# One core, two-layer trunk: two chunks of expert scores moved into the rank stage, one-hot products spread over 123 chunks, first expert loads moved into the gates stage

## The chip, the cores and the metric

The kernel runs on 1 core of one Trainium2 chip. The metric is the device time of one execution in microseconds (us), median over runs. TensorE (PE in the profile) does the matrix products, PEld is its weight load, VectorE (DVE), ScalarE (ACT) and GpSimd (POOL) do the elementwise work, and SyncE (SP) issues most of the DMA transfers. The kernel is written in five instruction streams, one for each engine, which meet only at semaphores and at the end of each stage: a stage is one block, and no engine starts the next block before all five have ended this one.

## The reference, cut to what matters

Two layers; each has a token mixer and then a PEER layer, which is where the change lies. There are 512 latent tokens and, in layer 0 alone, 256 context tokens as well. D is 1024, and there are 16384 experts on a grid of 128 x 128 keys.

```python
def peer_ffn(h, w_q, keys, u_tab, v_tab):
    q = (h @ w_q).reshape(bn, t, PEER_HEADS, 2, PEER_HALF)
    s = jnp.einsum('bthcd,hckd->bthck', q, keys)
    s_top, i_top = lax.top_k(s, PEER_TOPK)                       # rank stage
    cand_s = s_top[..., 0, :, None] + s_top[..., 1, None, :]
    cand_i = i_top[..., 0, :, None] * PEER_NKEYS + i_top[..., 1, None, :]
    best_s, pos = lax.top_k(cand_s.reshape(...), PEER_TOPK)      # gates stage: "select"
    idx = jnp.take_along_axis(cand_i, pos, axis=-1)
    gates = jax.nn.softmax(best_s, axis=-1)
    pre = einsum('ced,cd->ce', u_tab[idx], h)                    # 16 experts a head, 8 heads
    act = jax.nn.gelu(pre)
    return einsum('ce,ced->cd', act * gates, v_tab[idx])
```

## The kernel before

Of the tokens of a layer, most blocks of 128 are "dense": all 16384 expert activations are computed for them and multiplied by a gate that is zero for all but 128 experts. Layer 0 has 4 dense blocks (512 tokens) and 2 sparse ones, layer 1 has 3 dense ones (384 tokens) and 1 sparse. For sparse blocks only the chosen rows of the tables are gathered.

**stage_rank** makes the 16 query tiles and their scores on PE and ranks them on DVE. `t.product(pe, i, s, ...)` is one tile of product: 8 steps k, each of three matmuls (high weights by high tokens, high by low, low by high). ACT rounds a weight tile to its high part (`t.hi`), POOL in this stage, DVE in the next, makes the low part (`t.lo`); a product waits for `lo_done`, and for `acc_free`, which ACT gives when it has emptied the accumulator two tiles before.

**stage_gates** runs over 128 chunks c of 128 experts of the table u, of 8 steps each, so over 1024 positions p = 8c + k. All engines' streams are written out along p. At position p:

- PE does step k of chunk c, and ahead of it, at the positions of `group_at`, one group of 8 one-hot matmuls (L1124), which scatter the gates of 4 tokens into a 128 x 128 grid. `turn` (L1115) transposes the selections of a block, 12 positions ahead of the block's first group.
- DVE makes `low(c + 2)` where k = 0, the one-hots of the group that comes 14 positions later (L1008), a share of the row dots of the sparse blocks (`dots_to`, L985), and between these, in 13 pieces, the "select" of the block that `order` says (L1029 to L1096).
- ACT, after chunk c: `ahead(c)`, a gelu of the accumulator (L1146) that waits until the spill of chunk c - 2 has landed, then `hi(c + 3)`. Eight positions ahead of a group it scales the one-hots (`ojg`, L1160), two positions behind it copies the product to `stage` (L1169).
- SP loads the weight tile of chunk c + 4 (L131), stores 8 groups of gates at once (L1242, 2 MB), and spills chunk c's activations to `act_dram` (L1253). It is one queue in program order: a DMA whose issue takes long, or a wait, holds all behind it.

The groups start at chunk `lead` (16 and 20), and a block has `per` chunks (28 and 36), so the groups stand 7 positions apart in layer 0 and 9 in layer 1, and the last at position 1020 and 1019. At the end SP waits for all stores and spills.

**stage_experts** multiplies the activations by the gates (DVE, L1402), splits them (ACT L1374, DVE L1407) and multiplies them by the 128 chunks of the table v (PE, L1352 to L1354). It starts with SP's `quad_load(0)` (gates of the first 4 chunks, 1 MB in layer 0) and `act_load` of chunks 0 and 1. DVE also adds the gathered rows of v for the sparse blocks (L1416), which POOL fetches (L1333) after a memset (L1329).

## Time and profile before

| | us |
|---|---|
| median of the runs (4388.56 to 4394.6, 3 runs) | 4391.62 |
| the profiled execution, its own time | 4389.09 |
| its span in the trace | 4387.4 |
| PE busy in the span | 4032.8 (92%) |
| DVE busy in the span | 3231.5 (74%) |

The span is what the trace covers, the own time is measured around it. From the trace's rows, the stages of the PEER layer lie so: rank ends at about 662 and 3108, gates ends at about 1542 and 3794, experts ends at about 2279 and 4364.

### The profile page before, as it was taken

Reading aid. Unit: us, or ns where it says so; the run is one execution under the profiler, and the core shown is the slowest. Engines: PE = TensorE matmul, PEld = TensorE weight load, DVE = VectorE, ACT = ScalarE, POOL = GpSimd, SP = SyncE. Lnnn points to the kernel's source line nnn. Section 1 sums busy time; section 2 is a strip of 40 time slices with the busy share of each in tenths; the row PEclk is TensorE's granted clock in tenths of the full one; section 3 lists DMA queues with packets and bytes.
Section 4 is the critical chain, followed back from the end, with each engine's and each line's share of the span. In section 5 each row is a group of like instructions: output and inputs, shape, how many; then the busy total and the mean of one; then the engine's idle time right before and its main releaser. Section 6 shows DMA issues by size and latency. Waiting matters only on the chain. (4 is left out here: it accounts for less than half of the span.)

```text
span 4387.4 us, 62475 instructions
## 1 busy us (share of the span) xinstructions
PE 4032.8 (92%) x20380; PEld 3434.4 (78%) x20380; DVE 3231.5 (74%) x5929; ACT 1947.7 (44%) x3694; POOL 1163.9 (27%) x906
## 2 busy tenths in 40 slices
PE   8997788999999989999987999888799999899998
PEld 2776577788888868888866877656789999899997
DVE  2694588999897778888875455546887877577777
ACT  2111224777777722222224434323367778533332
POOL 0232121343343244444422111112122222122221
PEclk9998899999999999999998999889899999999999
DMA  7441115899999899999951111012378888899996
GB/s 278 169 168 58 44 43 183 284 326 335 318 344 332 316 386 375 373 374 376 376 196 49 38 38 39 29 48 77 123 270 285 285 281 300 293 333 333 331 336 213
DMA packets 411888, 1026.08 MB, mean 234 GB/s; under 512 B 33968, under 2 KB 182448, under 8 KB 405680
## 3 DMA queue, kind: packets, MB, share of 16 engines
q1 hardware_dynamic: 297648, 608.42, 39.0%
q0 software_dynamic: 110592, 402.70, 25.7%
q10 hardware_dynamic: 3456, 12.58, 0.9%
q8 instruction: 98, 1.61, 0.1%
q14 instruction: 94, 0.77, 0.1%
HBM read 904.03 MB, written 119.54 MB: 233 GB/s over the span
## 5 line engine op out<-in xcount | busy, mean ns | idle before, releaser
L136 ACT ACTIVATE w_hi<-w_raw 128x1024 fp32r<-128x1024 f32 x536 | 568.1, 1060 | 1197.9 <-PE psum L1354 879.8
L168 PE MATMUL psum<-h_hi,w_hi 128*128 128x512 f32 (+1 forms) x2208 | 876.4, 397 | 140.3 <-DMA keysr<-in_peer_keys 50.0
L169 PE MATMUL psum<-h_lo,w_hi 128*128 128x512 f32 (+1 forms) x2208 | 840.4, 381 | 0.0
L170 PE MATMUL psum<-h_hi,w_lo 128*128 128x512 f32 (+1 forms) x2208 | 839.7, 380 | 0.0
L147 DVE TENSOR_TENSOR w_lo<-w_raw,w_hi 128x1024 fp32r<-128x1024 f32 x424 | 519.5, 1225 | 413.3 <-ACT w_hi L136 392.2
L1352 PE MATMUL psum<-a_hie,w_hi 128*128 128x512 f32 (+1 forms) x2048 | 764.4, 373 | 30.7 <-DVE a_loe L1407 30.7
L1354 PE MATMUL psum<-a_hie,w_lo 128*128 128x512 f32 (+1 forms) x2048 | 751.6, 367 | 0.0
L1353 PE MATMUL psum<-a_loe,w_hi 128*128 128x512 f32 (+1 forms) x2048 | 750.0, 366 | 0.0
L1228 POOL DMA_INDIRECT u_rowsg<-in_peer_u_rows,expert_idx x384 | 443.4, 1155 | 1099.9 <-DVE u_rowsg L985 974.2
L1333 POOL DMA_INDIRECT v_rowse<-in_peer_v,expert_idx x384 | 421.4, 1097 | 828.2 <-DVE row_sume L1416 815.0
L1160 ACT ACTIVATE ojg<-eq_jg,gate_Tg 128x128 fp32r<-128x128 bf16 x1792 | 546.9, 388 | 167.5 <-DVE eq_jg L1008 166.6
L147 POOL TENSOR_TENSOR w_lo<-w_raw,w_hi 128x1024 fp32r<-128x1024 f32 x116 | 289.4, 2495 | 1145.2 <-ACT w_hi L136 1145.2
L168 PEld LDWEIGHTS psum<-h_hi,w_hi 128*128 128x128 f32 x2208 | 425.9, 193 | 195.5 <-issue 84.4
L1416 DVE SCALAR_TENSOR_TENSOR row_sume<-v_rowse,expert_weight,row_sume 128x1024 f32<-128x1024 f32 x384 | 491.4, 1280 | 0.1
L170 PEld LDWEIGHTS psum<-h_hi,w_lo 128*128 128x128 f32 x2208 | 424.3, 192 | 64.8
L985 DVE SCALAR_TENSOR_TENSOR u_rowsg<-u_rowsg,psum 128x1024 f32<-128x1024 f32 x384 | 463.1, 1216 | 9.5 <-DMA u_rowsg<-in_peer_u_rows,expert_idx 6.4
L169 PEld LDWEIGHTS psum<-h_lo,w_hi 128*128 128x128 f32 x2208 | 425.8, 193 | 49.0 <-issue 12.9
L1352 PEld LDWEIGHTS psum<-a_hie,w_hi 128*128 128x128 f32 x2048 | 385.7, 188 | 93.6 <-DVE a_loe L1407 31.8
L1354 PEld LDWEIGHTS psum<-a_hie,w_lo 128*128 128x128 f32 x2048 | 385.7, 188 | 50.4
L1353 PEld LDWEIGHTS psum<-a_loe,w_hi 128*128 128x128 f32 x2048 | 386.1, 189 | 45.9
L1124 PEld LDWEIGHTS psum<-ojg,eq_ig 128*128 128x128 f32 x1792 | 230.9, 192 | 78.8 <-ACT ojg L1160 70.1
L1124 PE MATMUL psum<-ojg,eq_ig 128*128 128x128 f32 x1792 | 232.6, 273 | 50.1 <-ACT ojg L1160 49.9
(228 smaller groups left out, 5740.2 us busy)
## 6 DMA issues: line engine op xcount, KB each, us to landing
w_raw<-in_peer_u SPq DMA_DIRECT2D x256, 512.0 KB, 5.9
w_raw<-in_peer_v SPq DMA_DIRECT2D x256, 512.0 KB, 5.5
gates<-stageg SPq DMA_DIRECT2D x28, 2048.0 KB, 15.7
acts<-act_gg SPq DMA_DIRECT2D x128, 256.0 KB, 5.0
gte<-gates SPq DMA_DIRECT2D x32, 1024.0 KB, 8.3
act_fe<-acts SPq DMA_DIRECT2D x128, 256.0 KB, 6.3
ada_w<-in_ada_w SPq DMA_DIRECT2D x12, 2048.0 KB, 8.2
ada_rows<-in_ada_w SPq DMA_DIRECT2D x48, 512.0 KB, 3.4
```

Of the source, the lines that this page charges most:

```text
L136: act.activation(self.weights(s)[0], self.raw[:, slot, :], ACT.Copy).then_inc(self.hi_done, 1)
L147: pool.tensor_tensor(lo, self.raw[:, slot, :], hi.bitcast(F32), ALU.subtract).then_inc(self.lo_done, 1)
L168: pe.matmul(out, wh, hi[:, k], start=(k == 0), stop=False)
L169: pe.matmul(out, wh, lo[:, k], start=False, stop=False)
L170: last = pe.matmul(out, wl, hi[:, k], start=False, stop=(k == KC - 1))
L985: dve.scalar_tensor_tensor(out=row, in0=row, scalar=1.0, in1=h_row, op0=ALU.mult, op1=ALU.mult, accum_out=pre_act[:, s, r:r + 1]).then_inc ...
L1124: last = pe.matmul(t.psum[:, 4 + g % 2, j * P:(j + 1) * P], eq_i[:, g % EQ, j], oj[:, g % OJ, x, j], start=(x == 0), stop=(x == 1))
L1160: last = act.activation(oj[:, g % OJ, x, j], eq_j[:, g % EQ, j], ACT.Copy, scale=gate_T[:, b % 2, x, r + j:r + j + 1])
L1352: pe.matmul(out, vh, a_hi[:, s], start=(begin and i == 0), stop=False)
L1353: pe.matmul(out, vh, a_lo[:, s], start=False, stop=False)
L1354: last = pe.matmul(out, vl, a_hi[:, s], start=False, stop=(end and i == QUAD - 1))
L1416: dve.scalar_tensor_tensor(out=acc[:, s], in0=vbuf[:, slot], scalar=weight[:, s, bass.ds(c, 1)], in1=acc[:, s], op0=ALU.mult, op1=ALU.add) ...
```

## The change

Three edits, in both layers.

1. At the end of stage_rank PE makes chunks 0 and 1 of the gates stage, over the dense tokens only: chunk 0 between the last query tile and the last scores, chunk 1 behind these. The PE loop of stage_gates starts at chunk 2. The work of ACT, DVE and SP for chunks 0 and 1 stays in stage_gates.
2. The groups of one-hot products are spread evenly from chunk `lead` to chunk 123: `span` is 856 positions for 128 groups in layer 0, which is 6.7 apart (before 7), and 824 for 96 groups in layer 1, 8.6 apart (before 9). The last group stands at 980 and 978; no group stands in the last five chunks. The ends of the selects move with the blocks: in layer 0 those behind the first dense block end at positions 199, 326, 540 and 754 (before 202, 336, 560 and 784).
3. The buffer `stage` now lives through both stages, and the expert stage's gate and activation buffers lie in it. SP, 12 positions behind the last store, waits until all stores have landed and then issues the loads of the first quad of gates and of activations 0 and 1, which stage_experts issued before.

```diff
+TAIL = 5
+ACTS = 4
...
                 for i in range(n - BODY, n):
                     if i + 1 < n:
                         t.product(pe, i + 1, (i + 1) % SPLIT, t.moving(tokens))
+                    else:
+                        t.wide = 1
+                        t.product(pe, n, 0, t.moving(tokens - S * P))
                     scores(i, i)
+                t.product(pe, n + 1, 1, t.moving(tokens - S * P))
+                t.wide = 2
...
-    per = (NKEYS - lead) // dense
     GB = P // 4
-    gap = per * KC // GB
+    span = (NKEYS - TAIL - lead) * KC
...
         def start(b):
-            return (lead + b * per) * KC
+            return lead * KC + b * span // dense
         def at(g):
-            return start(g // GB) + g % GB * gap + gap // 2
+            return lead * KC + g * span // (dense * GB) + 3
...
-                for c in range(NKEYS):
+                for c in range(SPLIT, NKEYS):
...
+                n = dense * STAGES
+                last_store = at(dense * GB - 1) + 4
                 for p in range(END):
                     if p % KC == 0:
                         load(p // KC + RAW)
+                    if p == last_store + 12:
+                        for x in range(2):
+                            sp.wait_ge(stored[x], 16 * (n // 2 + 1))
+                            sp.wait_ge(spilled[x], 32)
+                        gt, act_t = expert_buffers(stage, Td)
+                        sp.dma_start(gt[:, 0], g_dram[0].rearrange("i n x -> i (n x)")).then_inc(g_in, 16)
+                        for x in range(2):
+                            sp.dma_start(act_t[:, x], act_dram[x]).then_inc(act_in[x], 16)
...
-                if at(dense * GB - 1) + 4 >= END:
-                    store(dense * GB - 1)
-                n = dense * STAGES
                 for x in range(2):
                     sp.wait_ge(spilled[x], 16 * (NKEYS // 2 + 1))
-                    sp.wait_ge(stored[x], 16 * (n // 2 + 1))
...
+def expert_buffers(stage, Td):
+    halves = [stage[:, x].rearrange("p n x -> p (n x)") for x in range(2)]
+    return (halves[0][:, 0:2 * QUAD * Td].rearrange("p (a x) -> p a x", a=2),
+            halves[1][:, 0:ACTS * Td].rearrange("p (a x) -> p a x", a=ACTS))
...
                 sp.sem_inc(alo_done, A)
                 sp.sem_inc(gated, QUAD + 1)
-                quad_load(0)
-                act_load(0, 0)
-                act_load(1, 1)
```

On PE, at the end of layer 0's rank stage, before the change (L779 are the scores, L168 to L170 the three matmuls of a step, `hc_hip` and `hc_lop` the context tokens; the branches mark the change of block):

```order
L170 MATMUL psum<-hc_hip,w_lo 128x256
L779 MATMUL psum<-keysr,qTr 128x128 x12
L747 UNCONDITIONAL_BRANCH
L1107 UNCONDITIONAL_BRANCH
L168 MATMUL psum<-h_hi,w_hi 128x512
L169 MATMUL psum<-h_lo,w_hi 128x512
L170 MATMUL psum<-h_hi,w_lo 128x512
```

The same place with the change (lines are two higher there; the first "..." leaves out the rest of chunk 0, the second that of chunk 1):

```order
L172 MATMUL psum<-hc_hip,w_lo 128x256
L781 MATMUL psum<-keysr,qTr 128x128 x6
L170 MATMUL psum<-h_hi,w_hi 128x512
...
L781 MATMUL psum<-keysr,qTr 128x128 x6
L170 MATMUL psum<-h_hi,w_hi 128x512
...
L749 UNCONDITIONAL_BRANCH
L1113 UNCONDITIONAL_BRANCH
L170 MATMUL psum<-h_hi,w_hig 128x512
```

The 24 matmuls of chunk 0 now stand ahead of the last 6 score products and those of chunk 1 behind them, both ahead of the block's end; the next block starts with chunk 2, whose weights are in `w_hig` and `w_log`.

On SP, at the end of layer 0's gates stage and the start of its expert stage, before the change (`acts` are the spills, `gates` the stores, `gte` and `act_fe` the expert stage's loads):

```order
L1253 DMA acts<-act_gg 128x512
L131 DMA w_raw<-in_peer_v 128x1024
L1253 DMA acts<-act_gg 128x512
L1242 DMA gates<-stageg 128x32x128
L958 UNCONDITIONAL_BRANCH
L1291 UNCONDITIONAL_BRANCH
L1300 DMA gte<-gates 128x2048
L1295 DMA act_fe<-acts 128x512 x2
```

The same queue with the change, from the last store on (the spills are L1266, the first loads of the expert stage L1257 and L1259, its other loads of activations L1310):

```order
L1245 DMA gates<-stage 128x32x128
L1266 DMA acts<-act_gg 128x512
L133 DMA w_raw<-in_peer_v 128x1024
L1257 DMA stage<-gates 128x2048
L1259 DMA stage<-acts 128x512 x2
L1266 DMA acts<-act_gg 128x512
...
L133 DMA w_raw<-in_peer_v 128x1024
L1266 DMA acts<-act_gg 128x512
L964 UNCONDITIONAL_BRANCH
L1306 UNCONDITIONAL_BRANCH
```

The last store moved ahead of the last five spills, and the three loads now stand behind the store and the spill of chunk 123, and ahead of the spills of chunks 124 to 127.

## Rows read from the trace of the kernel before

**Rows 1.** The page: busy time, share of the span, instructions.
```profile
PE 4032.8 (92%) x20380; PEld 3434.4 (78%) x20380; DVE 3231.5 (74%) x5929; ACT 1947.7 (44%) x3694; POOL 1163.9 (27%) x906
```

**Rows 2.** Windows, gates stages: us, busy and count by engine, PE clock, DMA.
```profile
725.00:750.00 25.00, 19.55 (x85) 15.38 (x83) 24.07 (x51) 11.25 (x12) 8.77 (x6) 0.98 0.67 230
1425.00:1450.00 25.00, 25.00 (x127) 21.13 (x127) 22.18 (x34) 21.19 (x55) 9.09 (x9) 1.00 0.99 356
```

**Rows 3.** Windows, experts stage, layer 0.
```profile
2000.00:2050.00 50.00, 50.00 (x216) 40.23 (x215) 43.00 (x45) 14.23 (x18) 20.59 (x18) 1.00 0.99 379
```

**Rows 4.** Timeline of PE, rank to gates: start, us, [idle before <-releaser].
```profile
662.18 0.77 PE L168 MATMUL psum<-h_hi,w_hi 128*128 128x512 f32 x1 [15.78 <-PEq L747]
...
3108.24 0.66 PE L168 MATMUL psum<-h_hi,w_hi 128*128 128x384 f32 x1 [17.72 <-PEq L747]
```

**Rows 5.** Timeline, gates to experts, both layers.
```profile
1543.93 0.94 POOL L1333 DMA_INDIRECT v_rowse<-in_peer_v,expert_idx  x1 [0.15 <-issue]
1547.63 0.75 DVE L1402 TENSOR_TENSOR act_fe<-act_fe,gte 128x512 f32<-128x512 f32 x1 [11.45 <-DMA act_fe<-acts]
1549.83 0.80 PE L1352 MATMUL psum<-a_hie,w_hi 128*128 128x512 f32 x1 [17.30 <-DVE a_loe L1407]
...
3799.23 0.56 DVE L1402 TENSOR_TENSOR act_fe<-act_fe,gte 128x384 f32<-128x384 f32 x1 [8.36 <-DMA act_fe<-acts]
3800.99 0.69 PE L1352 MATMUL psum<-a_hie,w_hi 128*128 128x384 f32 x1 [13.35 <-DVE a_loe L1407]
```

**Rows 6.** Timeline of ACT, start of layer 0's gates stage.
```profile
664.63 1.28 ACT L1146 ACT_TABLE_LOAD   x1
670.14 0.60 ACT L1146 ACTIVATE act_gg<-psum 128x512 f32<-128x512 f32 x1 [4.23 <-PE psum L170]
670.91 1.06 ACT L136 ACTIVATE w_hi<-w_raw 128x1024 fp32r<-128x1024 f32 x1 [0.17 <-ACT act_gg L1146]
...
703.12 0.60 ACT L1146 ACTIVATE act_gg<-psum 128x512 f32<-128x512 f32 x1 [3.62 <-PE psum L170]
...
708.56 0.60 ACT L1146 ACTIVATE act_gg<-psum 128x512 f32<-128x512 f32 x1 [3.62 <-PE psum L170]
```

**Rows 7.** Timeline of DVE, first microseconds of the gates stages.
```profile
664.89 1.22 DVE L147 TENSOR_TENSOR w_log<-w_raw,w_hig 128x1024 fp32r<-128x1024 f32 x1
672.08 1.23 DVE L147 TENSOR_TENSOR w_lo<-w_raw,w_hi 128x1024 fp32r<-128x1024 f32 x1 [3.35 <-ACT w_hi L136]
...
699.60 1.23 DVE L147 TENSOR_TENSOR w_log<-w_raw,w_hig 128x1024 fp32r<-128x1024 f32 x1 [1.41 <-ACT w_hig L136]
...
3117.29 1.23 DVE L147 TENSOR_TENSOR w_lo<-w_raw,w_hi 128x1024 fp32r<-128x1024 f32 x1 [2.50 <-ACT w_hi L136]
```

**Rows 8.** Waits, 725 to 775 us: who <- whom, total, times, longest.
```profile
PE psum L1115 <- DVEq L1097: 7.6, 1, 7.6
```

**Rows 9.** Groups of instructions: the one-hot products (busy, mean | idle before).
```profile
L1124 PE MATMUL psum<-ojg,eq_ig 128*128 128x128 f32 x1792 | 232.6, 273 | 50.1 <-ACT ojg L1160 49.9
```

**Rows 10.** Line L958, end of both gates stages: count, duration, first to last start.
```profile
L958 DVEq DRAIN x2: 17/17/17, 1536.5 to 3791.1; - x2
L958 SPq DRAIN x2: 7/7/7, 1541.7 to 3794.0; - x2
```

**Rows 11.** Timeline of SP and ACT around a store, layer 0.
```profile
1486.77 0.45 SPq L1242 DMA_DIRECT2D gates<-stageg  x1
1492.09 11.26 SPq L1253 DMA_DIRECT2D acts<-act_gg  x1
...
1509.17 0.60 ACT L1146 ACTIVATE act_gg<-psum 128x512 f32<-128x512 f32 x1 [4.25 <-DMA acts<-act_gg]
```

**Rows 12.** Stores (L1242) from issue to landing: layer 0, all 16.
```profile
DMA to landing us min/median/max: 7.9/18.7/21.4
```

**Rows 13.** The same in layer 1, without its last store (11).
```profile
DMA to landing us min/median/max: 10.1/10.8/14.1
```

**Rows 14.** First gather of v (L1333, issued at 1543.93), to landing.
```profile
DMA to landing us min/median/max: 6.3/6.3/6.3
```

More of the change, by code:

```diff
@@ L871, in stage_rank, with stage_gates @@
         t.end_stage(n, RAW)
-def stage_gates(t, layer, tokens, top, top_i, h_tok, idx, weight, g_dram, act_dram):
+def stage_gates(t, layer, tokens, top, top_i, h_tok, idx, weight, g_dram, act_dram, stage):
     nc = t.nc
@@ L886, in stage_gates @@
     lead = LEAD[layer]
-    per = (NKEYS - lead) // dense
     GB = P // 4
-    gap = per * KC // GB
-    assert lead + dense * per == NKEYS and per * KC == gap * GB
+    span = (NKEYS - TAIL - lead) * KC
     tag = f"g{layer}"
@@ L917, in stage_gates @@
         oj = sb("oj", [P, OJ, 2, 4, P], F32R)
-        stage = sb("stage", [P, 2, NKEYS, STAGE_T])
         act_f = sb("act_g", [P, 2, Td])
+        g_in = t.sem("g_in" + tag)
+        act_in = [t.sem(f"act_in{x}{tag}") for x in range(ACTS)]
         ubuf = sb("u_rows", [P, UBUF, D])
@@ L947, in stage_gates @@
         for b in range(1, max(dense, S)):
-            order += [(start(b - 1) + per * KC // 3 * 2 // (2 if b < dense else 1), True, b)] if b < S else []
+            order += [(start(b - 1) + span // dense // 3 * 2 // (2 if b < dense else 1), True, b)] if b < S else []
             order += [(start(b) - 16, False, b)] if b < dense else []
@@ L1210, in _ @@
                         ahead(p // KC)
-                for g in range(dense * GB):
-                    if at(g) + 2 >= END:
-                        store_group(g)
                 for x in range(SPLIT):
@@ L1262, in stage_gates, with stage_experts @@
         t.end_stage(NKEYS, RAW)
-def stage_experts(t, layer, tokens, idx, weight, g_dram, act_dram, nxt=None):
+        return g_in, act_in
+def expert_buffers(stage, Td):
+    halves = [stage[:, x].rearrange("p n x -> p (n x)") for x in range(2)]
+    return (halves[0][:, 0:2 * QUAD * Td].rearrange("p (a x) -> p a x", a=2),
+            halves[1][:, 0:ACTS * Td].rearrange("p (a x) -> p a x", a=ACTS))
+def stage_experts(t, layer, tokens, idx, weight, g_dram, act_dram, stage, landed, nxt=None):
     nc = t.nc
@@ L1274, in stage_experts @@
     last_q = n // QUAD - 1
-    A = 4
+    A = ACTS
     with ExitStack() as ctx:
         sb = lambda nm, s, d=F32: ctx.enter_context(nc.sbuf_tensor(nm + tag, s, d))
-        gt = sb("gt", [P, 2, QUAD * Td])
-        act_f = sb("act_f", [P, A, Td])
+        gt, act_f = expert_buffers(stage, Td)
         a_hi = sb("a_hi", [P, 2, Td], F32R)
@@ L1283, in stage_experts @@
         acc = sb("row_sum", [P, S, D])
-        g_in = t.sem("g_in" + tag)
-        act_in = [t.sem(f"act_in{x}{tag}") for x in range(A)]
+        g_in, act_in = landed
         v_in, v_at = t.rows_in, list(t.rows_at)
@@ L1865, in hybrid_trunk @@
                 idx, weight = sb("expert_idx", [P, S, P], U32), sb("expert_weight", [P, S, P])
+                stage = sb("stage", [P, 2, NKEYS, STAGE_T])
                 with ExitStack() as lists:
@@ L1874, in hybrid_trunk @@
                         stage_rank(t, layer, tokens, top, top_i, h_tok, tile(f"peer_u{layer}"))
-                    stage_gates(t, layer, tokens, top, top_i, h_tok, idx, weight, g_dram[layer], act_dram[layer])
-                stage_experts(t, layer, tokens, idx, weight, g_dram[layer], act_dram[layer],
+                    landed = stage_gates(t, layer, tokens, top, top_i, h_tok, idx, weight, g_dram[layer],
+                                         act_dram[layer], stage)
+                stage_experts(t, layer, tokens, idx, weight, g_dram[layer], act_dram[layer], stage, landed,
                               tile("hgrn_w_in") if layer == 0 else None)
```

## The prediction

> **What bounds the kernel now.** I read the page's busy shares first: PE is busy 92% of the span and DVE 74% [rows 1]. That is an average over unlike stages, so next the windows. Early in layer 0's gates stage DVE is busy 24.07 of 25 us and PE only 19.55; late in the same stage PE is busy for all 25 and DVE for 22.18 [rows 2]. So the stage has two regimes: at first DVE sets the pace (select, low parts and dots, all in one order), later PE does. The expert stage is PE's throughout, 50.00 of 50 [rows 3]. Then the borders of the stages, in the timeline. From rank to gates PE stands 15.78 us in layer 0 and 17.72 us in layer 1 [rows 4], while DVE ranks the last two tiles. From gates to experts it stands 17.30 and 13.35 us [rows 5]. These four gaps, 64 us, are what the change can work on. What PE gains at the start of the expert stage reaches the end whole, since PE never waits in it; what it gains at the start of gates must first get past DVE.
>
> **Edit 1, two chunks made in the rank stage.** A chunk is 24 matmuls; two gelus follow each other at 703.12 and 708.56, so it takes 5.44 us at full clock in layer 0 [rows 6]. The two fit under the 15.78 us of waiting: chunk 0 needs 5.4 us ahead of the last scores, which comes to a delay of some 3.5 us of those scores, as PE had been waiting for ACT there. DVE needs these scores only after it has ranked the tile before, which takes it about 9 us. So I cost the delay at nothing; if DVE did wait, it would be up to 3.5 us a layer.
>
> What does it give? Before, chunk 2 began after chunks 0 and 1, at about 670.1 + 5.4 = 675.5. Now PE starts with chunk 2, which needs its low part, and that is DVE's at 664.89, ready at 666.1 [rows 7]. PE is thus 9.4 us ahead there. But DVE is the bound, and it can win no more than it stood idle. It stood 3.35 us before the low part of chunk 3, for ACT's high part, which came after the gelu of chunk 0 at 670.14 [rows 6, 7]. Now this gelu can follow the table load, at 664.63 + 1.28 = 665.9; with 0.6 for it and 1.2 for the high part (wait and all) the tile is there at 667.8, before DVE asks for it at 668.7. So the 3.35 go. The later waits, 1.41 us the longest [rows 7], depend on PE and on ACT, which itself waits for DVE in the select. I followed the chain: PE is held again at chunk 5 by the gelu of chunk 3, which stands behind ACT's copy for the select, and from there runs without a gap, so that chunk 7 ends at 702.9 where it ended at 708.5. I take 5.5 us; bounds 3.35 (only the first wait goes) and 7.3 (all six waits of that stretch do). From there DVE is busy without a break until PE's 7.6 us of waiting for the first block's selection [rows 8], so this shift is kept and nothing is added. In layer 1 the first wait is 2.50 us [rows 7]; the same chain gives 2.7 us, bounds 2.5 and 4.3. Sum of edit 1: -8.2 us, -5.9 to -11.6.
>
> **Edit 2, the groups closer together.** The number of one-hot products stays 1792 and costs PE 232.6 us in any place [rows 9]. What changes is when. In the part of layer 0 where DVE is the bound, DVE gets about one more group by position 256 (19.2 for 18.3, at 1.2 us) and a slightly denser select: I estimate +2.3 us, of which PE gets 0.8 back later, when DVE has slack. So +1.5 us. In layer 1 DVE has more slack: 0. At the tail the last groups and the store no longer fall on the last chunks, where PE waited for the scaled one-hots for some 4 us in both layers together; part of such waits is only moved, so -2.5 us. PE's waits for these one-hots are 49.9 us in all [rows 9], and a changed spacing can shift them either way: I give -3 to +6 for the spreading and 0 to -3.8 for the tail.
>
> **Edit 3, the first quad fetched early.** Before, the gates stage ended when the 2 MB store had landed: DVE was through at 1536.5 and 3791.1, SP only at 1541.7 and 3794.0 [rows 10]. After that DVE's first gate waited for its loads until 1547.63 and 3799.23, and PE began 2.2 and 1.8 us behind it [rows 5]. With store and loads gone from there, what ends last is DVE's tail; the last spill then has no store beside it and should land before. The new start of PE is then 1536.5 + 0.3 for the border + 0.1 + 2.2 = 1539.1 in place of 1549.83, and 3791.1 + 0.2 + 0.1 + 1.8 = 3793.2 in place of 3800.99. That is -10.7 and -7.8.
>
> Three things come against it. First, SP's queue. A 2 MB store fills it: with store and spill in the same phase of the chunk as the last ones will have (store at 1486.77, position 968), the spill behind it took 11.26 us to issue, and ACT's gelu waited for its landing until 1509.17, which is 22.4 us after the store [rows 11]. In the new layer 0 this gelu is that of chunk 125, and PE, with no groups left to do, wants its accumulator four chunks after position 984, near which the store is issued: some 20 us after it, so 2.9 us of stall with the gelu's own time. Behind it SP waits for the store itself (18.7 us, up to 21.4 [rows 12]), then issues 1.5 MB, and only then the spill of chunk 124, which holds the gelus of chunks 126 and 127 by some 1.5 us. I take +4 us, 0 to 6.3. In layer 1 stores land in 10.8 us [rows 13] and chunks are shorter; by the same count the spills are just in time: 0, up to +2. Second, the gathered rows of v: POOL's memset and first gather start only with the stage, and the first row lands 6.3 us after its issue at 1543.93 [rows 5, 14]. DVE now meets it before it has landed, and the low part for chunk 1 stands behind it: +0.3 in layer 0, where chunk 0 takes PE as long, and +1.3 in layer 1. Third, PE's clock is at its lower level after such gaps in both kernels, so I change nothing for it. Sum of edit 3: -6.4 in layer 0 (-4.4 to -10.7) and -6.5 in layer 1 (-4.5 to -7.8).
>
> The store's landing shows how much the transfers disturb each other: 7.9 us for the last one, where nothing else runs, and 21.4 at the most, next to the gathers [rows 12]. The Trainium skill, DMA: Bandwidth & Descriptors, Queues, rings and completion order, says that each DMA engine goes round the queue rows that have work and takes the descriptors of one ring in order. By this rule a spill behind the early loads waits for all 1.5 MB in SP's ring, and the page's 6.15 us for 1 MB would make some 9 us of it, an estimate, and the sum 5 us smaller than mine.
>
> **Sum.** -8.2 + 1.5 - 2.5 - 6.4 - 6.5 = -22.1 us. Against the profiled execution's own time of 4389.09 that is 4367.0. This execution is 2.5 us below the median of the runs, 4391.62, so for the median I say 4369.5. All bounds together give -9 to -37 us, that is 4355 to 4383.
>
> **The rivals.**
> - *PE's time counts in full* (0.10). If DVE's slack is larger than its busy time shows, PE's lead of 9.4 us in layer 0 and about 7 in layer 1 is kept, and the queue costs nothing: -9.4 - 7 - 10.7 - 7.8 - 2.5, about -37 us, 4354. Against it: DVE at 24.07 of 25 [rows 2].
> - *DVE takes edit 1 whole* (0.15). The stage is paced by DVE and its early waits only move to the next tile. Then edit 1 gives nothing and 14 us are left: 4378. For it: PE's wait at the first turn [rows 8] exists already and would grow. A rule of the Trainium skill leads here too: Perfetto Trace Analysis, Identifying the Most-Contended Engine, says to find the engine with the highest occupancy and improve that first. In this stretch it is DVE, and the change takes no work from it.
> - *The early loads come late* (0.05). They sit behind a store that lands in 21.4 us at worst [rows 12]. If all of edit 3's gain in waiting for data (5.6 us a layer) went, the time would be 4381.
> - *Closer groups make PE wait* (0.07), the other side. DVE makes one-hots 14 positions ahead but must not run past the group two before; in layer 0 this was 14 positions back and is now 13 or 14, so every late step passes on to ACT and PE. There are 224 groups and PE waits 49.9 us for them, 0.22 us each [rows 9]. At 0.32 us each the gain is gone, from 0.36 the kernel is slower by over 0.2%. At 0.42 it loses 45 us: 4415. Against it: late in the stage DVE and ACT have 3 to 4 us of slack in 25 [rows 2].
>
> **How the numbers follow.** My forecast has 0.63. The range of 8 in 10 takes its bounds and leans to the side of the second and third rival: 4355 to 4386. A difference of 0.2%, 8.8 us, is about what a measurement can tell from no change. Below 4382.8 lie the forecast nearly whole, the first two rivals and part of the third: 0.84 faster. Above 4400.4 lies the last rival: 0.05. Between them 0.11.
>
> **What the new profile would show.** PE's gap from rank to gates split by two chunks, with about 11 us left before its first matmul of the gates stage, released by DVE's low part; no wait of 3.35 us on DVE before the second low part; PE's wait at the first turn about as long as before. From gates to experts a gap of 7 to 9 us, the stage ended by DVE's drain and not by SP's, and the first gate right behind the border. A long spill behind the last store and a wait of ACT for it in layer 0. Waits for one-hots near 50 us in all. The prediction is wrong if DVE's first select does not end earlier, if these waits grow, or if the last spills hold the end of the stage.

## The result, and the profile after

The changed kernel took 4402.34 us (median of 15 runs, 4394.67 to 4414.83), the kernel before 4390.32 us in the same series. The ratio is 1.0034 with a 95% interval of 1.0023 to 1.0045: about 15 us slower by the ratio, 12 us between the two medians, where 22 us faster was forecast. The profiled execution took 4405.64 us (span 4403.9).

The page of the changed kernel, its busy times and the row of the one-hot products on PE:

```profile
PE 4054.6 (92%) x20380; PEld 3454.4 (78%) x20380; DVE 3233.9 (73%) x5929; ACT 1945.8 (44%) x3694; POOL 1151.9 (26%) x906
...
L1130 PE MATMUL psum<-ojg,eq_ig 128*128 128x128 f32 x1792 | 236.4, 276 | 67.3 <-ACT ojg L1166 67.1
```

PE waits 67.1 us for scaled one-hots where it waited 49.9 [rows 9]. The borders of the stages did what edit 3 was to do. The timeline of the changed kernel, from gates to experts, layer 0 and then layer 1:

```profile
1541.00 1.80 POOL L1341 MEMSET row_sume<- 128x2048 f32 x1 [22.18 <-POOLq L964]
1541.10 0.69 DVE L1414 TENSOR_TENSOR stage<-stage 128x512 f32<-128x512 f32 x1 [1.02 <-PEq L964]
1543.24 0.80 PE L1364 MATMUL psum<-a_hie,w_hi 128*128 128x512 f32 x1 [7.96 <-DVE a_loe L1419]
...
1551.07 1.28 DVE L1428 SCALAR_TENSOR_TENSOR row_sume<-v_rowse,expert_weight,row_sume 128x1024 f32<-128x1024 f32 x1 [5.91 <-DMA v_rowse<-in_peer_v,expert_idx]
...
1553.01 0.51 PE L1364 MATMUL psum<-a_hie,w_hi 128*128 128x512 f32 x1 [1.28 <-DVE a_loe L1419]
...
3815.60 0.69 PE L1364 MATMUL psum<-a_hie,w_hi 128*128 128x384 f32 x1 [5.60 <-DVE a_loe L1419]
...
3824.26 0.45 PE L1364 MATMUL psum<-a_hie,w_hi 128*128 128x384 f32 x1 [2.70 <-DVE a_loe L1419]
```

PE stands 7.96 and 5.60 us there, for 17.30 and 13.35 [rows 5]; DVE has its first operands 0.1 us after the border. Then a second wait follows that the kernel before did not have, 1.28 and 2.70 us: DVE stands 5.91 us for the first gathered row of v, and the low part of chunk 1 stands behind it.

Most of the loss is inside layer 1's gates stage. The windows from the gelu of chunk 16 to that of chunk 127, kernel before and then the changed one (same 3444 matmuls):

```profile
3188.59:3787.68 599.09, 567.56 (x3444) 557.95 (x3442) 451.02 (x741) 452.51 (x1095) 137.64 (x121) 0.99 0.83 281
```

```profile
3179.85:3810.03 630.18, 582.57 (x3444) 569.43 (x3442) 451.74 (x741) 451.22 (x1094) 136.44 (x121) 0.96 0.82 271
```

Columns are length, busy PE, PEld, DVE, ACT, POOL, PE's granted clock, DMA share, GB/s. The stretch is 31.1 us longer. Of that PE is idle 16.1 us more and busy 15.0 us more for the same work, at a mean granted clock of 0.96 in place of 0.99. In layer 0 the same stretch went from 761.0 to 769.5 us: chunks 16 to 60 took 323.5 us for 310.9, and the rest was 4.2 us shorter. Who PE and ACT waited for in layer 1's gates, first before, then the changed kernel (us in total, times, longest):

```profile
PE psum L1124 <- ACT ojg L1160: 26.9, 23, 2.1
...
ACT act_gg L1146 <- DMA acts<-act_gg: 4.4, 5, 1.7
```

```profile
PE psum L1130 <- ACT ojg L1166: 43.4, 34, 5.0
...
ACT act_gg L1152 <- DMA acts<-act_gg: 31.9, 9, 4.9
```

The wait for one-hots makes up all of the added idle time (+16.5 us). ACT's gelu waits 31.9 us for a spill to land, seven times as long as before. One store in the changed kernel, SP's queue first, then ACT, then PE:

```profile
3349.70 0.39 SPq L1245 DMA_DIRECT2D gates<-stage  x1
3350.13 7.45 SPq L1266 DMA_DIRECT2D acts<-act_gg  x1
3357.62 1.25 SPq L133 DMA_DIRECT2D w_raw<-in_peer_u  x1
...
3363.53 0.49 ACT L1152 ACTIVATE act_gg<-psum 128x384 f32<-128x384 f32 x1 [4.87 <-DMA acts<-act_gg]
3364.53 1.06 ACT L138 ACTIVATE w_hig<-w_raw 128x1024 fp32r<-128x1024 f32 x1 [0.51 <-DMA w_raw<-in_peer_u]
3365.49 2.43 ACT L1166 ACTIVATE ojg<-eq_jg,gate_Tg 128x128 fp32r<-128x128 bf16 x8
...
3367.98 1.68 PE L1130 MATMUL psum<-ojg,eq_ig 128*128 128x128 f32 x8 [2.49 <-ACT ojg L1166]
...
3370.20 0.52 PE L172 MATMUL psum<-h_hi,w_lo 128*128 128x384 f32 x1
3370.52 0.52 PE L170 MATMUL psum<-h_hi,w_hi 128*128 128x384 f32 x1
```

The spill behind the store takes 7.45 us to issue, the gelu waits 4.87 us, and the scaling of the next group stands behind the gelu; PE waits 2.49 us for it, and its matmuls then stand 0.32 us apart for 2 us, as at 1.2 GHz, where they otherwise stand 0.17 apart, as at 2.4 GHz. The long issue as such is not new: before, the spill behind a store of layer 1 took 4.5 to 7.4 us to issue too (without the last one), and 3.2 to 9.3 with the change. What is new is where in the chunk it falls.

What edit 2 changed about this was not seen in the prediction. Eight groups make a store. Before, eight groups took exactly 56 positions in layer 0 and 72 in layer 1, whole chunks, so each store stood at one position of its chunk (0 and 7), and the n-th group after a store always at the same one too. With 6.7 and 8.6 positions this relation drifts. I state two theories. A: the place of the store against spill and load decides, through the gelu's wait. B: the closer groups as such cost it.

### The profile page after: what moved, and what is told of

The parts are those of the page before. It is cut to its first block and busy times, and to the rows that moved or that the text cites. A ratio compares the mean times of both kernels' runs of the same rounds, so it can differ in the third digit from the quotient of the medians.

```text
span 4403.9 us, 62480 instructions
## 1 busy us (share of the span) xinstructions
PE 4054.6 (92%) x20380; PEld 3454.4 (78%) x20380; DVE 3233.9 (73%) x5929; ACT 1945.8 (44%) x3694; POOL 1151.9 (26%) x906
## 5 line engine op out<-in xcount | busy, mean ns | idle before, releaser
L170 PE MATMUL psum<-h_hi,w_hi 128*128 128x512 f32 (+1 forms) x2208 | 878.8, 398 | 105.8 <-DMA keysr<-in_peer_keys 50.1
L1231 POOL DMA_INDIRECT u_rowsg<-in_peer_u_rows,expert_idx x384 | 428.0, 1115 | 1142.9 <-DVE u_rowsg L991 1013.6
L170 PEld LDWEIGHTS psum<-h_hi,w_hi 128*128 128x128 f32 x2208 | 427.9, 194 | 160.5 <-DMA keysr<-in_peer_keys 51.3
L1130 PE MATMUL psum<-ojg,eq_ig 128*128 128x128 f32 x1792 | 236.4, 276 | 67.3 <-ACT ojg L1166 67.1
```

Source lines behind the costliest of these rows:

```text
L170: pe.matmul(out, wh, hi[:, k], start=(k == 0), stop=False)
L1130: last = pe.matmul(t.psum[:, 4 + g % 2, j * P:(j + 1) * P], eq_i[:, g % EQ, j], oj[:, g % OJ, x, j], start=(x == 0), stop=(x == 1))
```

## The experiments

All times below are medians, with the ratio to the kernel before (4386 to 4391 us in these series) and its 95% interval.

**Taking the change apart.** e1_rank_chunks is the kernel before with edit 1 alone, e2_spread with edit 2 alone, and e3_no_rank_chunks is the changed kernel without edit 1; they are the hunks of the diff above and nothing else.

> The kernel before with edit 1 alone (chunks 0 and 1 at the end of the rank stage; groups, stores and loads as before). Both theories of the loss put it into edit 2, so both expect what the prediction gave for edit 1: about -8 us (0.998 of before), of it -5.5 in layer 0 and -2.7 in layer 1, and gates stages whose waits for stores and spills are those of before. If edit 1 itself brought the loss (PE's clock after a gap that is split by two chunks, say), it would be +10 to +25 us here.

> The kernel before with edit 2 alone (groups spread over 123 chunks; chunks 0 and 1 and the experts' loads where they were). Both theories: the whole loss is here, +20 to +35 us (1.005 to 1.008), nearly all of it in layer 1's gates stage, since the prediction's gains of edits 1 and 3 (about 21 us, of which the front of the stages and the borders show most) are missing. They differ in the cause: theory A (stores of 2 MB now meet every phase of a chunk, ACT's gelu waits for spills behind them, PE waits and its clock falls) expects ACT's waits for a landed spill in layer 1 to be near 30 us in place of 4.4; theory B (closer groups, DVE's and ACT's order alone) expects them near 5 and longer waits for one-hots only. If the prediction's sizes for edit 2 hold, -1 us.

> The changed kernel without edit 1 (edits 2 and 3 stay). If edit 1 gives what the prediction said, this is 8 us slower than the changed kernel: 1.005 of before, about 4410. If the gain of edit 1 is lost again later in the stage (its shift lets stores and spills meet otherwise), it is within 3 us of the changed kernel.

Measured: edit 1 alone 4385.65 (0.9995, 0.9986 to 1.0003), edit 2 alone 4418.05 (1.0071, 1.0058 to 1.0084), edits 2 and 3 4418.52 (1.0072, 1.0059 to 1.0085). So edit 2 alone loses 31 us, edit 3 adds nothing that can be measured to that, and edit 1 brought 16 us beside the others but only about 2 alone. In edit 2's trace both gates stages are longer between first and last gelu, 862.4 to 875.4 us and 672.2 to 698.0 us.

**Where the store stands.** In store_after_spill SP issues each store right behind the spill of its chunk. In spill_buffers, layer 1 has four buffers for the gelu's result.

```
-                    g = group_at.get(p - 4, 0)
-                    if g % STAGE_G == STAGE_G - 1:
-                        store(g)
...
                         sp.dma_start(act_dram[c], act_f[:, c % 2]).then_inc(spilled[c % 2], 16)
+                        for q in range(p - KC + 1, p + 1):
+                            g = group_at.get(q - 4, 0)
+                            if g % STAGE_G == STAGE_G - 1:
+                                store(g)
```

```
+GELU_BUFS = (2, 4)
...
-                    act.wait_ge(spilled[c % 2], 16 * (c // 2 + 1))
+                    act.wait_ge(spilled[c % GELUS], 16 * (c // GELUS + 1))
```

> The changed kernel, but SP issues a 2 MB store right behind the spill of its chunk, so no spill ever stands behind a store by less than a chunk. Theory A (the phase of the store against the spill): ACT's waits for landed spills in layer 1's gates fall from 31.9 us to under 10, PE's stretches at the low clock there from 68 us to about 25, and the time by 15 to 30 us, to 4372 to 4387. Theory B (density of the groups): no change, within 4 us of the changed kernel.

> The changed kernel with four buffers in place of two for the gelu's result in layer 1's gates (layer 0 has no room for them). If the gelu's wait for a landed spill is what holds ACT, the one-hots and PE, layer 1's 31.9 us of such waits go, its gates stage gets 15 to 30 us shorter and the time comes to about 4375 to 4388. If the closer groups themselves cost the time, or if the store holds up something else as well (the loads of the weights), the time stays within 6 us of 4402 though the waits for spills go.

Measured: 4461.87 (1.0166, 1.0153 to 1.0179) and 4407.31 (1.0041, 1.0027 to 1.0055). Theory A in this form fell. ACT's waits in layer 1's gates (3180 to 3800 us), store_after_spill and then spill_buffers:

```profile
ACT w_hi L138 <- DMA w_raw<-in_peer_u: 24.2, 6, 6.4
ACT w_hig L138 <- DMA w_raw<-in_peer_u: 17.4, 4, 6.4
```

```profile
ACT w_hi L139 <- DMA w_raw<-in_peer_u: 19.4, 6, 5.7
ACT w_hig L139 <- DMA w_raw<-in_peer_u: 14.6, 4, 5.0
```

The gelu's waits are nearly gone in both (none in the second), but ACT now waits 41.6 and 34.0 us for the raw weights, where the changed kernel waits 12.2 in the same window. The store holds up whatever SP issues next: with the spill out of the way it is the load. The Trainium skill, Perfetto Trace Analysis, Optimization Strategy, says that the same gap repeating on the engine that should be saturated can mean too few buffers for the next tile. Here the repeated gap was ACT's, which is not that engine, and the runs give no gain: two more buffers took the wait of 31.9 us away and the kernel became no faster.

**The order spill, load, store.** store_behind_load issues a store only at position 0, behind the load; both_mended adds the four buffers. before_phase is the kernel before with every group 3 (layer 0) or 4 (layer 1) positions later, which leaves density and spacing alone. before_l1_later leaves even the groups alone and issues layer 1's stores at position 0 in place of 7.

```
# store_behind_load
-                    g = group_at.get(p - 4, 0)
-                    if g % STAGE_G == STAGE_G - 1:
-                        store(g)
+                    for q in range(p - KC + 1, p + 1) if p % KC == 0 else ():
+                        g = group_at.get(q - 4, 0)
+                        if g % STAGE_G == STAGE_G - 1:
+                            store(g)
# before_phase
-            return start(g // GB) + g % GB * gap + gap // 2
+            return start(g // GB) + g % GB * gap + gap // 2 + 3 + layer
# before_l1_later
-                    g = group_at.get(p - 4, 0)
+                    g = group_at.get(p - 4 - layer, 0)
...
-                if at(dense * GB - 1) + 4 >= END:
+                if at(dense * GB - 1) + 4 + layer >= END:
```

> The changed kernel, but SP issues a 2 MB store only right behind the load that opens a chunk (position 0 of 8), so the order is always spill, load, store, as it was for every store of layer 0 before. The run with the store between spill and load showed 110.9 us of PE's waits for one-hots and 41.6 us of ACT's waits for weights in layer 1 in place of 12. If the place of the store in SP's queue is the cause, the waits for weights fall back to 12 us, PE's waits for one-hots to about 50, and the time to 4370 to 4385. If it is the density of the groups, it stays near 4402.

> Both edits of the two kernels before this one: store behind the load and four gelu buffers in layer 1. If the store's collisions with spills and loads cost the whole loss, 4365 to 4380, and at least as fast as each alone. If density is the cause, 4395 to 4405.

> The kernel before with every group 3 positions later in layer 0 and 4 in layer 1, so density, spacing and sizes are those of before and only the phase of group and store in a chunk is another one (position 3 of 8 in place of 0 in layer 0, and 3 in place of 7 in layer 1). If the phase of the store decides, ACT's waits for spills rise from 24 us to 50 or more and the kernel loses 10 to 30 us (1.002 to 1.007). If density or the changing spacing is the cause, it stays within 0.2% of before.

> The kernel before with one change: in layer 1 SP issues every store one position later, behind the next chunk's load, in place of just ahead of the spill (position 0 for 7). Density is that of before. If the place in SP's queue decides in layer 1 too, its gates stage grows by the 5 to 15 us that the store-behind-load run still showed over before there (687.4 for 672.2 us between first and last gelu), to 4393 to 4403. If those 15 us are the closer groups', it stays at before.

Measured: 4384.75 (0.9992, 0.9983 to 1.0001), 4387.19 (1.0000, 0.9991 to 1.0009), 4429.29 (1.0095, 1.0080 to 1.0111) and 4383.27 (0.9988, 0.9979 to 0.9997). Moving groups and stores by 3 positions in layer 0 and 4 in layer 1 costs the kernel before 42 us, more than the whole change, at unchanged density (29.7 us between first and last gelu in layer 0, 17.8 in layer 1); putting the changed kernel's stores behind the load gives 18 back. Position 0 is no worse than 7 in layer 1. That before_phase moved groups and stores together left open which of the two counts; I had it down as the store.

**The change with the old relation kept.** kept_phase has all three edits, but spaces the groups 7 and 9 positions apart as before, and only the last 40 of a layer one position closer. That keeps every store at its old position (8 groups in 48 and in 64 positions, whole chunks again) and still ends 5 chunks early. It has a side effect that was not meant: layer 1's last 40 groups stand 8 apart, and all of them at position 3. kept_phase_no_rank leaves out edit 1, kept_tail_alone edits 1 and 3.

```
+        def at_group(g):
+
+            return g * gap - max(0, g + 1 - (dense * GB - TAIL * KC))
...
-            return lead * KC + g * span // (dense * GB) + 3
+            return lead * KC + at_group(g) + gap // 2
```

> All three edits, but the groups keep the spacing of the kernel before (7 and 9 positions) except the last 40 of each layer, which stand one position closer, so every store stands at the position in its chunk that it had before (0 in layer 0, 7 in layer 1) and the last one still comes 5 chunks early. If the phase of the stores is what the forecast missed, the rest of it now shows: 15 to 22 us faster than before, 4365 to 4373. If closer groups as such cost the time, only part of them is closer here: 4385 to 4400.

> The same without edit 1. Against the kernel above it gives edit 1's worth beside kept phases: the prediction said 8.2 us, edit 1 alone measured 2 with an interval of -1 to 6; with the last groups' stores in place 3 to 8 is expected, so 4371 to 4379.

> The kernel before with that spacing alone (no edit 1, no early loads): the last store no longer ends the stage. The gap from gates to experts falls by about 5 us in layer 0 and 3 in layer 1 (as in the run with edit 2 alone: 12.0 and 10.5 us from the last gelu in place of 17.3 and 13.3), the rest of both gates stages is as before: 4378 to 4384. If closer groups cost time as such, it is at or above before.

Measured: 4369.05 (0.9960, 0.9944 to 0.9976), 4373.31 (0.9968, 0.9955 to 0.9981), 4372.26 (0.9965, 0.9955 to 0.9976). The forecast of 4369.5 happens to fit this kernel. The spacing alone carries 15 of the 19 us. Edit 3 on top of it is worth nothing that can be measured (+1), and edit 1 about 4, which with these intervals is not clear of nothing either.

**Density against position.** kept_later is kept_phase with layer 1's stores at position 0. dense_layer1 then sets layer 1's groups 8 positions apart throughout, one in every chunk at position 3; dense_group_phase moves them to position 7, and with them all that hangs on a group (DVE's one-hots, ACT's scaling and copy); dense_store_phase moves only the stores, to position 4.

```
# dense_layer1
-            return g * gap - max(0, g + 1 - (dense * GB - TAIL * KC))
+            return g * gap - max(0, g + 1 - (0 if layer else dense * GB - TAIL * KC))
# dense_group_phase (stores kept at position 0)
-            return lead * KC + at_group(g) + gap // 2
+            return lead * KC + at_group(g) + gap // 2 + 4 * layer
# dense_group_phase and dense_store_phase
-                    g = group_at.get(p - 4 - layer, 0)
+                    g = group_at.get(p - 4 - 5 * layer, 0)
```

> The kernel with all three edits and kept phases, with layer 1's stores one position later as in the run that did this alone (663.0 us from first to last gelu in place of 672.2, and waits for spills of 1.1 in place of 4.4). There the border behind the stage took 2.5 us of it back, since the last store ended the stage; here no store is at the end. Expected: layer 1's gates stage 3 to 9 us shorter than with kept phases, 4360 to 4367. If the gain of that run was only its scatter, the time is 4366 to 4372.

> The kernel above with layer 1's 96 groups 8 positions apart throughout (one in each chunk, 12.5% closer than before, where the changed kernel's are 4.9% closer), stores still at position 0 of a chunk. This tells density from phase: if closer groups cost time by themselves, at the changed kernel's rate of some 15 to 20 us for 4.9% layer 1 now loses 20 to 50 us to the kernel above. If only the phases cost, it is within 6 us of it.

> The kernel with one group in each of layer 1's chunks, but its one-hot products at position 7 of the chunk in place of 3; stores stay at position 0. If it is the group's position in its chunk that decides whether ACT has scaled the one-hots in time (at position 7 the next group's scaling falls on the gelu), PE's waits for them in layer 1 rise from 3.6 us towards 25 or more and the time by 10 to 30 us, to 4347 to 4367. If only that the position is the same in every chunk counts, it stays within 5 us of 4337.

> The same kernel with the groups at position 3 as in the fast run, but layer 1's stores at position 4 of a chunk in place of 0. If the store's position costs by itself, as it did with the spacing of before moved by 4 positions (690.0 us from first to last gelu for 672.2), the time rises by 10 to 20 us, to 4347 to 4357. If a store only costs where the groups have no slack against it, it stays within 5 us of 4337.

Measured: 4359.5 (0.9932, 0.9919 to 0.9946), 4337.02 (0.9888, 0.9871 to 0.9904), 4487.35 (1.0233, 1.0219 to 1.0247), 4337.28 (0.9885, 0.9869 to 0.9900). Theory B, that closer groups cost time by being closer, is refuted: with 12.5% more groups per chunk than before, the kernel is faster than every one above. The group's position in its chunk is worth 150 us in one layer, far over my 10 to 30; the store's position, with groups at 3, nothing. PE's waits for one-hots in layer 1, dense_layer1 and then dense_group_phase:

```profile
PE psum L1135 <- ACT ojg L1171: 3.6, 6, 1.8
```

```profile
PE psum L1135 <- ACT ojg L1171: 111.3, 88, 4.5
```

And what a chunk looks like with the group at position 7 (timeline of dense_group_phase, DVE's rows and then ACT's):

```profile
3407.82 1.23 DVE L149 TENSOR_TENSOR w_lo<-w_raw,w_hi 128x1024 fp32r<-128x1024 f32 x1 [2.97 <-ACT w_hi L138]
3408.96 0.68 DVE L1019 TENSOR_TENSOR eq_ig<-iota,psum 128x512 fp32r<-128x512 f32 x1
3409.56 0.68 DVE L1019 TENSOR_TENSOR eq_jg<-iota,psum 128x512 bf16<-128x512 f32 x1
```

```profile
3406.09 0.47 ACT L1157 ACTIVATE act_gg<-psum 128x384 f32<-128x384 f32 x1
3406.73 1.06 ACT L138 ACTIVATE w_hi<-w_raw 128x1024 fp32r<-128x1024 f32 x1 [0.17 <-ACT act_gg L1157]
...
3410.27 2.45 ACT L1171 ACTIVATE ojg<-eq_jg,gate_Tg 128x128 fp32r<-128x128 bf16 x8 [2.00 <-DVE eq_jg L1019]
3412.63 0.47 ACT L1157 ACTIVATE act_gg<-psum 128x384 f32<-128x384 f32 x1
```

This is a closed ring: gelu, high part, DVE's low part, DVE's one-hots, their scaling, and the next gelu, which stands behind the scaling in ACT's program. One turn takes 3412.63 - 3406.09 = 6.54 us, while PE's work of a chunk is 24 matmuls 0.173 us apart and a group of 1.0, some 5.2 us. A ring that is longer than the chunk sets the pace. The whole stretch agrees with this one turn (gelu of chunk 16 to that of chunk 127, dense_layer1 and then dense_group_phase, columns as above):

```profile
3167.00:3737.69 570.69, 559.76 (x3444) 555.75 (x3442) 451.01 (x739) 448.74 (x1094) 129.72 (x121) 0.99 0.90 299
```

```profile
3170.04:3890.80 720.76, 594.26 (x3444) 564.53 (x3442) 451.08 (x739) 453.37 (x1094) 124.17 (x121) 0.97 0.73 237
```

These are 111 chunks, so 5.14 us each and 6.49 us each, near PE's own work in the first and near one turn of the ring in the second; DVE's waits for ACT's high parts of u went from 109.5 to 260.1 us. At position 3 the scaling comes half a chunk after the gelu and the ring is open. That the position is what counts is shown by the run; that it counts through this ring is read from the traces, and no run took a single link out of it. The Trainium skill, PSUM — Partial Sum Buffer, Engine vs sequencer instructions, says that the queues of ScalarE, VectorE and GpSimdE are strict FIFO; the trace agrees, the gelu starts only as the 2.45 us of scaling end.

With this I sorted PE's waits for one-hots by the position of their group (the n-th group of products in PE's timeline against the n-th place of the program; us in total):

```
position in the chunk          0     1     2     3     4     5     6     7
before, layer 1             12.7   1.0   0     0     0     0     0.6  12.6
before_phase, layer 1       12.2   0.7   0    16.1   1.2   0     1.1   5.4
changed kernel, layer 1     14.1   1.2   4.9   2.1   2.1   0.4   9.7   8.9
store_behind_load, layer 1  12.6   0.5   1.9   1.6   0     0     9.9   9.0
before_l1_later, layer 1    13.3   1.0   0     0     0     0     0.5   3.5
before, layer 0              2.4   1.4   1.1   0.2   2.5   0.7  12.8   2.0
before_phase, layer 0        0     0.3  27.9   1.9   1.9   0.2   4.0   1.3
```

Two kinds of waits lie on top of each other. Groups at 0 wait in layer 1 in every one of these kernels, 1.0 to 1.2 us each; those at 7 wait less by themselves, 0.3 us each in before_l1_later and 0.5 in before_phase. The other kind stands behind a store: in the changed kernel's layer 1 the four waits of over 0.9 us at positions 2, 3 and 4 come 18 to 25 us after a store's issue, and in before_phase all seven at position 3 do, 18 to 20 us after. Before, the delay behind a store met PE 20 to 22 us after it at position 7 and passed positions 1 to 6 by; with the stores one position later, behind the load, the waits at 7 fall from 12.6 to 3.5 us. In before_phase it always meets position 3 (layer 1) or 2 (layer 0), and in the changed kernel every position in turn. This does not explain all of the 16.5 us. At position 6 PE waits 9.7 us, where it waited 0.6 before, and still 9.9 in store_behind_load; of the waits of over 0.9 us there, two come 24 us after a store, the others 5, 31 and 38 us after one. So the spacing of 8.6 costs something of its own at these positions, which no run took apart.

**Layer 0 by the same rule.** There 8 groups must fit into 7 chunks; placed_layer0 puts six at position 3 and two at 1 and 5 of one chunk, in place of a spacing of 7 (near the end of the layer, where 8 groups fall into 6 chunks, four and four).

```
+PLACES = (1, 5, 11, 19, 27, 35, 43, 51)
+LATE = (1, 5, 11, 19, 25, 29, 35, 43)
...
+            s, i = divmod(g, 8)
+            return lead * KC + 56 * s - KC * max(0, s - 11) + (PLACES if s < 11 else LATE)[i]
```

> The fast kernel (one group in each of layer 1's chunks, at position 3) and in layer 0, where eight groups must fit into seven chunks, groups at position 3 of six chunks and at 1 and 5 of the seventh in place of a spacing of 7. If groups at positions 6, 7 and 0 are what PE waits for, most of layer 0's 20 us of waits for one-hots go, and with them 8 to 20 us of time: 4317 to 4329. If layer 0 is bound by DVE anyway, the waits only move: within 5 us of 4337. The two groups of one chunk stand 4 positions apart; if that is what costs, it is slower.

Measured: 4338.1 (0.9887, 0.9867 to 0.9907), the same as dense_layer1. PE's waits for one-hots in layer 0 fell from 20.4 to 14.0 us, and the time between first and last gelu stayed (860.1 and 859.0). The rule of positions does not pay in layer 0; that this is because DVE paces the stage is argued from [rows 2], not shown by a run.

## Why the prediction was wrong

- **Edit 2 is the step that failed.** It was costed at +1.5 for the spreading ("In layer 1 DVE has more slack: 0") and -2.5 for the tail. Alone it measured +31 us. In layer 0, where the estimate for DVE was 2.3 us up to chunk 32, the changed kernel lost 4.6 us from chunk 16 to 32 and 12.6 up to chunk 60. Over these 44 chunks DVE's own work is 4.4 us more, but it also stood 16.1 us for ACT's high parts where it stood 6.1, and ACT's gelu stood 8.8 us for spills where it stood 0.8. The argument asked how busy DVE and ACT are over 25 us, and PE does not wait for the average: it waits at certain positions of the chunk, and behind stores. The text even said that "a changed spacing can shift them either way", with -3 to +6; in layer 1 the waits rose by 16.5 and in the page as a whole by 17.2. The tail's idea was right and too small: with the old relation kept, closing the last 40 groups gave 15 us, for the 2.5 there and the about 8 of edit 3's sum that the borders show with edit 2 alone. In layer 1 part of it may be the position: those 40 groups all stand at 3, where PE waited 0.3 us for them together in kept_tail_alone.
- **The rival "Closer groups make PE wait"** (0.07) named the place and not the cause: the waits grew from 0.22 to 0.30 us a group. By its own table even 0.32 would only have cancelled the gain. What it left out is the clock. PE was busy 15.0 us longer in the windows above for the same matmuls, beside 16.1 us of added idle time. That is this one trace; in the same stretch of the others the busy time rose less for each microsecond of added idle time: by 0.5 with edit 2 alone (8.5 for 16.0), 0.3 in e3_no_rank_chunks (6.4 for 19.3), 0.7 in spill_buffers (11.6 for 16.0), and 0.3 from dense_layer1 to dense_group_phase (34.5 for 115.6). And "closer" was not the cause, as dense_layer1 shows.
- **Edit 1**, forecast -8.2: in the traces it does what was said. DVE's waits of 3.35 and 2.50 us [rows 7] are gone. Counted from DVE's first instruction of the gates stage (its cast to `row_ofg`), the gelu of chunk 16 comes after 103.5 us for 109.5 in layer 0 and after 78.0 for 80.5 in layer 1, together the forecast's size; in layer 0 the runs with edit 1 show 103.5 to 103.7 (placed_layer0 105.0), those without it 109.5 or more. PE's gap before the gates is 11.56 and 14.32 us behind the two chunks. What comes after takes it back or adds to it: the runs give 2 us alone, 4 beside kept_phase and 16 in the changed kernel. The 2 and the 16 differ by more than their intervals, that of the 4 overlaps both. I take it that the shift changes where stores and groups meet, but no run shows that.
- **Edit 3**, forecast -12.9: PE's new starts behind the border are right: its first product comes 2.24 and 1.87 us after the first row of the new stage (1541.00 and 3813.73), where 2.3 and 1.9 were forecast. But edit 2 alone, whose last store no longer ends the stage, had taken much of it already: last gelu to PE's first product is 17.3 us before, 12.0 with edit 2 alone and 6.8 with edit 3 (layer 1: 13.3, 10.5, 5.6). Of the 10 us that were left for it, nothing measurable remained. SP's queue does hold the last spills of layer 0 (ACT waits 6.82, 6.50 and 1.28 us for them), and in layer 1, where 0, up to +2, was costed, ACT waits 4.18 and 3.87; but PE, costed with 2.9 us of stall in layer 0, has no wait over 0.3 us in the last chunks of either. (The bound of -4.4 us in layer 0 leaves out its own 0.3 for the v rows; it should read -4.1.) What fell short is the start of the expert stage. The v rows were costed at 0.3 and 1.3 us and cost 1.28 and 2.70: in the first 25 us of the expert stage PE got through 89 matmuls in layer 0 for 98 before, and 107 in layer 1 for 124. At 0.23 and 0.18 us each that is 2 and 3 us, mostly those waits; less than 1 us a layer is left for PE's clock, so "I change nothing for it" was nearly right.

The two windows of the changed kernel (length, PE's busy time and matmuls, PE's granted clock, DMA share, GB/s):

```profile
1543.24:1568.24 25.00, 23.72 (x89) 0.88 1.02 398
3815.60:3840.60 25.00, 22.30 (x107) 0.87 0.95 340
```

The kernel before, whose PE never waits there:

```profile
1549.83:1574.83 25.00, 25.00 (x98) 0.91 1.03 408
3800.99:3825.99 25.00, 25.00 (x124) 0.88 0.98 352
```

From PE's first to its last product the expert stages took 721.2 and 559.4 us in the changed kernel, for 719.1 and 556.5 before. In e3_no_rank_chunks they took 722.9 and 560.3, for 718.8 and 556.1 with edit 2 alone: 8.3 us lost behind the borders, of the 9.3 us that the borders themselves gave there (with the old relation kept, kept_phase_no_rank against kept_tail_alone, 5.8 of 9.4).

- **The sum.** With the spreading taken back the total comes near the forecast: kept_phase measured 18.7 us below before, where 22.1 were forecast. But this is mostly luck, since the tail gave 15 us for 2.5, edit 3 nothing that can be measured for 12.9, and edit 1 about 4 for 8.2.

Open stay: how edit 1 can be worth 2 us alone and 16 in the changed kernel; and why the order spill, load, store leaves layer 1's gates at 687.4 us in the changed kernel and at 663.0 in before_l1_later. The table of positions says where: 17.1 us more waits for one-hots, 9.4 of them at position 6 and 5.5 at 7. The drift of the group's position against the store differs between them, and so does the spacing, but neither was varied alone.

## What to carry to other kernels

When several engines run hand-interleaved programs of a fixed period (here a chunk of 8 positions), ask at which position of the period each extra piece of work falls, and follow one turn of the loop through all in-order queues: a ring longer than the period sets the pace, whatever the busy shares say. Before spacing work evenly over a stretch, look whether the old spacing was a whole multiple of the period; an uneven spacing visits the bad positions, and one piece per period at a good position (4337 us) beat both the old and the new spacing. Price a wait of PE at 1.3 to 1.9 times its length where its clock falls after it, as these traces show it, and a transfer that moves to another place in a queue by what is issued right behind it.

## What the runs showed of the hardware

- The issue of a 256 KB transfer on SP's queue behind a 2 MB store took 7.45 us in the rows above (3.2 to 9.3 over the stores of layer 1), and 0.34 us where no store stood ahead; in the changed kernel the stores' median landing is 14.0 us. The delay passes to whichever transfer comes next: spills (31.9 us of ACT's waits), or, when these have buffers, loads (34.0 us).
- PE's mean granted clock fell with waits of 1 to 5 us spread over a stage, but not in a fixed ratio: 0.99 in layer 1's gates with 27 us of waits for one-hots before, 0.96 with 43 in the changed kernel, 0.97 with 43 in spill_buffers, 0.98 with 48 in e3_no_rank_chunks, 0.97 with 111 in dense_group_phase. The added busy time was 0.3 to 0.9 us for each added microsecond of idle time.
- Moving 96 groups (1.0 us of PE's work each, with 1.3 us of DVE's and 2.45 us of ACT's that belong to them) by four positions of the program moved the kernel by 150 us (4337.02 to 4487.35), with every engine's amount of work unchanged.
